# Attention row sums moved from TensorE to GpSimd for four of eight heads, with three other moves, in a one-core encoder kernel

## What is computed

```python
def attend(q_blk):
    s = jnp.einsum('bqhd,bkhd->bhqk', q_blk, k).astype(jnp.float32) * scale
    prob = jax.nn.softmax(s, axis=-1)
    return jnp.einsum('bhqk,bkhd->bqhd', prob.astype(v.dtype), v)
...
sa = jnp.einsum('bhvk,bhk->bhv', S, a_t)
S_new = S * w_t[:, :, None, :] + sa[..., None] * b_t[:, :, None, :] + v_t[..., None] * k_t[:, :, None, :]
```

## Time and profile before

| | us |
|---|---|
| three runs | 1579.66, 1581.14, 1581.53 |
| median | 1581.14 |
| the profiled execution, its time | 1581.29 |
| its span in the profile | 1579.4 |
| TensorE busy | 1525.7 (97%) |
| VectorE busy | 1051.0 (67%) |
| ScalarE busy | 636.6 (40%) |
| GpSimd busy | 349.3 (22%) |
| mean granted TensorE clock | 0.995 of full speed |

### The profile page before, as it was taken

One profiled execution on the slowest core, in us unless ns is written; L12 is line 12 of the kernel. 1 busy time (PEld: TensorE's weight loads), 2 busy tenths in 40 slices (PEclk: granted clock), 3 DMA queues, 4 the chain that ended last, 5 costly groups with the idle time before them and its releaser, 6 DMA issues.

```text
span 1579.4 us, 25838 instructions
## 1 busy us (share of the span) xinstructions
PE 1525.7 (97%) x10160; PEld 1104.2 (70%) x10160; DVE 1051.0 (67%) x1503; ACT 636.6 (40%) x1178; POOL 349.3 (22%) x356
## 2 busy tenths in 40 slices
PE   6999999999999999999999999999999999999998
PEld 5888776644555546777764457888888888888786
DVE  6424589678666676666548489875555555689877
ACT  5212247645444444444430125433333333343553
POOL 0810013146100028887830050220000000000000
PEclk9999999999999999999999999999999999999999
DMA  6141020010000000000033011333221111765322
GB/s 244 45 155 53 20 63 5 7 28 13 12 12 24 7 18 16 2 2 29 2 129 126 1 53 54 114 115 118 81 80 54 54 54 54 260 207 196 124 67 107
DMA packets 29001, 110.70 MB, mean 70 GB/s; under 512 B 3568, under 2 KB 6096, under 8 KB 26720
## 3 DMA queue, kind: packets, MB, share of 16 engines
q1 hardware_dynamic: 28432, 103.97, 19.5%
q0 software_dynamic: 464, 5.28, 0.8%
HBM read 89.36 MB, written 18.92 MB: 69 GB/s over the span
## 4 chain that ended last, share of the span: by engine, by line
PE 72%; issue 12%; DVE 9%; POOL 5%; ACT 2%; DMA 1%; DVEq 0%; SPq 0%; POOLq 0%; ACTq 0%
PE psum L2909 25%; PE psum L2926 12%; PE psum L2833 7%; PE psum L2579 4%; PE psum L2606 3%; PE psum L2497 2%; PE psum L2613 1%; PE psum L2516 1%; PE psum L2467 1%; POOL arena L853 1%; POOL arena L855 1%; PE psum L2807 1%; PE psum L2720 1%; PE psum L2716 1%; PE psum L2702 1%
## 5 line engine op out<-in xcount | busy, mean ns | idle before, releaser
L1988 DVE TENSOR_TENSOR part_lo<-arena,part_hi 128x512 fp32r<-128x512 f32 x154 | 117.7, 768 | 77.2 <-ACT part_hi L1269 77.0
L2909 PE MATMUL psum<-h_hi,part_hi 128*128 128x512 f32 x616 | 165.7, 391 | 1.1 <-ACT arena L1317 0.7
L2909 PE MATMUL psum<-h_lo,part_hi 128*128 128x512 f32 x616 | 164.7, 389 | 0.0
L2909 PE MATMUL psum<-h_hi,part_lo 128*128 128x512 f32 x616 | 164.7, 389 | 0.0
L1269 ACT ACTIVATE part_hi<-arena 128x512 fp32r<-128x512 f32 x154 | 95.9, 628 | 133.3 <-PE psum L2909 114.8
L2909 PEld LDWEIGHTS psum<-h_hi,part_hi 128*128 128x128 f32 x616 | 115.2, 188 | 26.7 <-ACT arena L1317 1.1
L2909 PEld LDWEIGHTS psum<-h_lo,part_hi 128*128 128x128 f32 x616 | 115.6, 188 | 24.1
L2909 PEld LDWEIGHTS psum<-h_hi,part_lo 128*128 128x128 f32 x616 | 115.6, 188 | 24.0
L919 POOL TENSOR_TENSOR arena<-arena,consts 128x512 f32<-128x512 f32 x64 | 81.8, 1299 | 179.9 <-ACT arena L1170 179.3
L1658 DVE TENSOR_REDUCE stats<-psum 128x1 f32<-128x1024 f32 x64 | 77.8, 1216 | 51.1 <-PE psum L2497 51.0
L2833 PE MATMUL psum<-arena 128*128 128x512 f32 x256 | 110.5, 592 | 0.0
(11 more groups left out here) (329 smaller groups left out, 3046.7 us busy)
## 6 DMA issues: line engine op xcount, KB each, us to landing
arena<-in_w_gate SPq DMA_DIRECT2D x22, 512.0 KB, 3.7
arena<-in_w_up SPq DMA_DIRECT2D x22, 512.0 KB, 3.8
arena<-in_w_down SPq DMA_DIRECT2D x22, 512.0 KB, 3.7
arena<-in_w_down SPq DMA_DIRECT2D x11, 1024.0 KB, 4.9
arena<-in_w_in SPq DMA_DIRECT2D x15, 512.0 KB, 3.5
arena<-act_spill SPq DMA_DIRECT2D x12, 512.0 KB, 7.1
act_spill<-arena SPq DMA_DIRECT2D x10, 512.0 KB, 6.1
arena<-in_x SPq DMA_DIRECT2D x8, 512.0 KB, 8.5
```

Of the source, the lines that this page charges most:

```text
L1988: v.tensor_tensor(lo, raw[:, at:at + HALF], hi, ALU.subtract).then_inc(part_lo, 1)
L2909: mm = pe.matmul(bank({2: z, 3: y, 5: y}.get(p, x)), w[:, P * k:P * k + P], h[k // 2][:, HALF * (k % 2):HALF * (k % 2) + HALF], start=(fre ...
```

## The change

Four edits:

1. **Sums.** For heads 4 to 7, GpSimd adds the exponentials of the eight key tiles elementwise into one 128x1024 buffer (`e_sums`): seven additions a head, counted by `summed`. In head 7 it adds six tiles (five additions). TensorE then needs four matmuls with ones for a whole head (`sums_of`) in place of 64, between scores 0 and 1 of the next head; for head 7 it runs them ahead of `values` 6, and the last two tiles are added by TensorE as before. ScalarE now also waits for `summed` ahead of writing a ring buffer. VectorE inverts the sums of heads 4 to 6 when scores 1 of the next head are done. The loops over these heads are written out on PE, ACT and DVE.
2. **Decayed operands.** `At` and `Rt` of `q` 0 and 1 are made in head 6, behind the row maxima 3 and 4 (`decayed`), and no longer in head 7.
3. **GpSimd's order.** The five operations of `q` now wait for the first scores of head `q`.
4. **Start.** The identity matrix is loaded behind the first four row tiles.

```diff
@@ -295,6 +295,8 @@
+        SUMMED = 4
+        e_sums = [reg(X0 + 6144, T), reg(WK0 + 3200, T)]
...
@@ -643,8 +645,7 @@
         def _(sp):
             for t in range(4):
                 sp.dma_start(resid[:, t, :], a["x"][t]).then_inc(rows_in_place[t], 16)
-                if t == 0:
-                    sp.dma_start(ident, a["consts"][:, 0:P]).then_inc(ident_in, 16)
+            sp.dma_start(ident, a["consts"][:, 0:P]).then_inc(ident_in, 16)
             for s in range(NSLOT):
...
             pool.wait_ge(z_sig, 14)
             pool.wait_ge(kk_ready, 2)
-            pool.wait_ge(s_done, 1)
             for q in range(4):
                 hp = q % 2
+                pool.wait_ge(s_done, 8 * q + 1)
                 own.add(pool.tensor_tensor(Bt[:, q], Kt[:, q], kk[:, hp], ALU.mult))
                 own.wait()
                 own.add(pool.tensor_scalar(Kt[:, q], Kt[:, q], pcol("k_a", hp), one_less_ka[:, hp:hp + 1],
@@ -907,6 +908,15 @@
                 own.add(pool.tensor_tensor(Bt[:, q], Bt[:, q], half[q % 2], ALU.mult))
                 own.wait()
                 pool.tensor_tensor(Kt[:, q], Kt[:, q], half[q % 2], ALU.mult).then_inc(kb_ready, 1)
+
+            pool.wait_ge(kb_ready, 4)
+            for n in range(HEADS - SUMMED):
+                total = e_sums[n % 2]
+                for kt in range(1, NT if n < HEADS - SUMMED - 1 else NT - 2):
+                    pool.wait_ge(e_ready, 8 * (SUMMED + n) + kt + 1)
+                    if kt > 1:
+                        pool.wait_ge(summed, 7 * n + kt - 1)
+                    pool.tensor_tensor(total, e_ring[0] if kt == 1 else total, e_ring[kt % NE], ALU.add).then_inc(summed, 1)
 
             pool.wait_ge(prods_ready, PRODS[3])
             def level(d, m, i):
...
@@ -1170,13 +1180,17 @@
...
-            def head_exps(i, b, ahead, ahead2, with_decays=False, last=False):
+            def head_exps(i, b, ahead, ahead2, with_decays=False, last=False, add_up=False):
...
                         act.wait_ge(pv_done, 8 * i + (4 * b + (kt - NE) // 2 + 1))
+                    if add_up and (kt >= NE or first_summed < 2 * i + b):
+                        n = 2 * i + b - first_summed
+                        act.wait_ge(summed, 7 * n + max(kt - NE, 1) if kt >= NE else 7 * (n - 1) + kt + NE)
                     at = 2 * (1 - kt % 2)
                     act.activation(halves(e_ring[kt % NE]), psum[:, at:at + 2, :], ACT.Exp, scale=MLA_SCALE).then_inc(e_ready, 1)
                 if ahead:
...
@@ -1721,9 +1735,12 @@
                         row_max(*nxt, kt)
                     beside(kt)
 
-            def invert(i, b, last=False):
-
-                v.wait_ge(pv_done, 8 * i + (4 * b + 4))
+            def invert(i, b, last=False, add_up=False):
+
+                if add_up and 2 * i + b < HEADS - 1:
+                    v.wait_ge(s_done, 8 * (2 * i + b + 1) + 2)
+                else:
+                    v.wait_ge(pv_done, 8 * i + (4 * b + 4))
                 v.reciprocal(inv_own[last][b], bank(7, 256)).then_inc(inverted, 1)
 
             def scale_pair(i, last=False):
...
 
-            def recurrence_operands():
-
-                v.wait_ge(max_ready, HEADS)
+            def decayed(q):
+
+                hp = q % 2
+                v.wait_ge(pr_q, HEADS)
                 v.wait_ge(pr_v, HEADS)
-                v.wait_ge(s_done, 8 * (HEADS - 1))
                 v.wait_ge(kb_ready, 4)
                 v.wait_ge(ex_ready, 16)
+                if q < 2:
+                    v.tensor_tensor(by_chunk(At[:, q])[:, :, 0], by_chunk(kk[:, hp])[:, :, 0], lead[:, q],
+                                    ALU.mult).then_inc(prods_ready, 1)
+                    v.tensor_tensor(by_chunk(At[:, q])[:, :, 1:P], by_chunk(Rt[:, q])[:, :, 0:P - 1],
+                                    by_chunk(kk[:, hp])[:, :, 1:P], ALU.mult).then_inc(prods_ready, 1)
+                else:
+                    v.tensor_tensor(At[:, q], Rt[:, q], kk[:, hp], ALU.mult).then_inc(prods_ready, 1)
+                v.wait_ge(prods_ready, PRODS[q] - 1)
+                v.tensor_tensor(Rt[:, q], Rt[:, q], r_sh[:, hp], ALU.mult).then_inc(prods_ready, 1)
+
+            def recurrence_operands():
+
+                v.wait_ge(max_ready, HEADS)
+                v.wait_ge(s_done, 8 * (HEADS - 1))
                 for q in range(4):
                     hp = q % 2
-                    if q < 2:
-                        v.tensor_tensor(by_chunk(At[:, q])[:, :, 0], by_chunk(kk[:, hp])[:, :, 0], lead[:, q],
-                                        ALU.mult).then_inc(prods_ready, 1)
-                        v.tensor_tensor(by_chunk(At[:, q])[:, :, 1:P], by_chunk(Rt[:, q])[:, :, 0:P - 1],
-                                        by_chunk(kk[:, hp])[:, :, 1:P], ALU.mult).then_inc(prods_ready, 1)
+                    if q >= 2:
+                        decayed(q)
                     else:
-                        v.tensor_tensor(At[:, q], Rt[:, q], kk[:, hp], ALU.mult).then_inc(prods_ready, 1)
-                    v.wait_ge(prods_ready, PRODS[q] - 1)
-                    v.tensor_tensor(Rt[:, q], Rt[:, q], r_sh[:, hp], ALU.mult).then_inc(prods_ready, 1)
-                    if q < 2:
-                        v.wait_ge(prods_ready, PRODS[q])
+                        v.wait_ge(prods_ready, PRODS[1])
                         v.scalar_tensor_tensor(out=bonus[hp], in0=Kt[:, q], scalar=pcol("r_k", hp), in1=Rt[:, q],
                                                op0=ALU.mult, op1=ALU.mult).then_inc(rk_ready, 1)
 
...
+                        invert(i, 0, last=True, add_up=True)
                         recurrence_operands()
...
-            def values(i, b, first):
+            def sums_of(i, b):
+
+                last = 2 * i + b == HEADS - 1
+                pe.wait_ge(summed, 7 * (2 * i + b - SUMMED + 1) - 2 * last)
+                pe.wait_ge(inverted, 2 * i + (b + 2))
+                for g in range(4):
+                    mm = pe.matmul(bank(7, 256, slice(32 * g, 32 * g + 32)), cst(C_ONES)[:, 0:32],
+                                   e_sums[b][:, 256 * g:256 * g + 256], start=True, stop=not last, skip_group_check=True)
+
+            def values(i, b, first, add_up=False):
...
+                if first == 0 and not add_up:
                     pe.wait_ge(inverted, 2 * i + (b + 2))
-                for kt in (first, first + 1):
+                for kt in () if add_up and (i, b, first) != (HEADS // 2 - 1, 1, 6) else (first, first + 1):
                     for g in range(4):
...
                 scores(i, b, 0, ahead)
+                if left_over is not None:
+                    sums_of(*left_over)
                 scores(i, b, 1, ahead)
...
                     pe.wait_ge(e_ready, 8 * HEADS)
                     attention(PLAN[1])
-                values(i, b, 6)
+                    sums_of(i, b)
+                values(i, b, 6, add_up)
...
-            with pe.Fori(0, HEADS // 2 - 1) as i:
+            with pe.Fori(0, SUMMED // 2) as i:
                 for b in range(2):
                     head(i, b, True, True)
-            for b in range(2):
-                head(HEADS // 2 - 1, b, b == 0, False)
+            for h in range(SUMMED, HEADS):
+                before = ((h - 1) // 2, (h - 1) % 2) if h > SUMMED else None
+                head(h // 2, h % 2, h < HEADS - 1, h < HEADS - 2, add_up=True, left_over=before)
```

More of the change, by code:

```diff
@@ L1816, in _ @@
             pair(0, None)
[L1817 to L1820 removed]
+            for i in range(1, HEADS // 2 - 1):
+                pair(i, i - 1)
             pair(HEADS // 2 - 1, HEADS // 2 - 2, last=True)
```

42 lines of the change are left out of this document (20 added, 22 removed).

## The result

The changed kernel takes 1585.82 us (median of seven runs, 1582.23 to 1587.40); the kernel before, run beside it, 1580.11 (seven, 1576.88 to 1582.40). The ratio is 1.0039, 95% interval 1.0028 to 1.0049: 6 us slower, where 1582.6 was forecast. That is within the range, but on the slow side of the 0.2% that the prediction called no change. The profiled execution took 1585.09 with a span of 1583.3, 3.9 more than before.

The account below looks back on a forecast made before the run. TensorE's instruction stream (72% of the span) was taken to set the pace. Heads 4 and 5, head 6, head 7, clock, order, start: -6.6 + 3.7 + 7.5 + 3.2 - 6.0 - 0.5 = +1.3 on 1581.29, so 1582.6; range 1568 to 1591.

Parts of the forecast that it names:

- who holds whom: Latent attention: two-SBUF-input VectorE instructions and GpSimd's never run together; they alternate at 1.1 us and 1.9 us a sum.
- VectorE is not held twice: Rival, chance 0.28: head 6 loses 2.5 instead of 6.0, head 7's operands end at 14 instead of 21; 1570.
- heads 4 and 5, -6.6 predicted: Each head 33.10 - 3.67 for fewer ones + 0.35 for late guard 3 = 29.8, so -6.6 for two.
- head 6, +5.3 with its clock: Head 6: the same saving, less cover 0.98 and 6.0 for decayed operands: 32.0, +3.7, before the clock's share.
- its clock: Heads 6 and 7: TensorE at 1.2 GHz behind new waits, two stretches, +3.2 together (0 to 5).
- The early keys themselves: Head 6: decayed operands between row maxima 3 and 5 take guards 3 to 7 to 15.7 against 10.1; 6.0 taken.
- the dear-sums rival: Rival, chance 0.16: a GpSimd sum takes 2.2 or more, delaying guards 4 and head 7; +5.8, clock +1.5, 1590.
- Head 7, +7.5 and 1.6 of clock predicted: Head 7: VectorE's operands, alternating with five sums, end at 21; the first chunk's second block at 30.3, before 22.0; +7.5.
- The 0.8 that was taken off for the second block: Head 7: some 0.8 that GpSimd took from the second block before, taken off +8.3 to give +7.5.
- the order and the start: GpSimd's order in heads 1 and 2, -6.0 (-3 to -7.5); identity load at the start, -0.5 (0 to -1).
- the price that was put on head 1 for `q` 1: Head 1: VectorE still waits for two products of `q` 1, making guards 5 and 6 late by 1.1 together.
- the 0.8 kept for chance: Order term of heads 1 and 2: 0.8 for a chance of a slow stretch, within the -6.0.

Follow-up runs that it names:

- writes_only: The changed kernel with GpSimd's additions replaced by fills of the same buffer, which read nothing: 1565.83 us, ratio 0.9909.
- The swaps: Two kernels, the kernel before with GpSimd's two residual operations exchanged, or their gain and bias rows instead: 2.00 us with the bias row, 2.40 with the gain row.
- sums_4to6_late: The changed kernel with sums in heads 4 to 6 only, decayed operands back in head 7, VectorE's turned-query split behind row maxima 3: 1565.83 us, ratio 0.9912.
- order_only: The kernel before with only GpSimd's order changed, each q waiting for the first scores of head q: 1572.49 us, ratio 0.9955.
- start_only: The kernel before with only the identity matrix loaded behind the first four row tiles: 1576.78 us, ratio 0.9986.
- order_start: The kernel before with both GpSimd's new order and the later identity load, no sums and no early keys: 1571.39 us, ratio 0.9952.
- decayed_in_7: The changed kernel with the decayed operands of q 0 and 1 made in head 7 again: 1583.01 us, ratio 1.0025.

## Why the prediction went as it did

**Right: who holds whom.** VectorE and GpSimd took turns for as long as both had work: 3.1 to 3.4 us a pair in head 7, `attention(PLAN[1])` waiting for VectorE (3.90), one decayed instruction of 3.25 in head 6, the clock under 0.97 in both heads, heads 1 and 2 clean. "VectorE is not held twice" is out by the same rows, and writes_only shows that the loss lies in GpSimd's reading additions: their turns with VectorE and, not separated from them, their length. The Trainium skill ("SBUF — State Buffer", Who interferes with whom) gives the rule that was used; each row above agrees with it.

**Wrong: heads 4 and 5, -6.6 predicted, -3.3 measured.** Three numbers of this step failed, of which the first is the large one: guard 4's waits, 1.12 and 0.88, are 2.0 of the 3.3.
- A sum was priced at 2.00, from the earlier trace rows, because the row there was the same operation. The swaps show that the operation had nothing to do with it. A sum in the heads costs 2.38 (median of 26), as the products of the earlier trace rows do. Then the third sum ends beyond the point where the scores 4 and 5 hide VectorE's subtraction, and guard 4 is 1.1 late. The step said that these scores hide it, also for a wait of up to 1.9. That does not come out of its own numbers: 1.9, 1.1 for the subtraction and 1.2 for the row maximum are 4.2, and from guard 3 to where guard 4 could start are 3.5 (464.67 to 468.19). sums_4to6_late, where the wait is gone, has heads 4 and 5 at 30.03 and 30.76, beside the predicted 29.8.
- `sums_of` was priced at 0.25, a quarter of a group of ones. A group is eight calls of `matmul`, which the trace counts as x16, and `sums_of` is four: half a group. From scores 0 to scores 1 head 5 takes 2.17 with it and head 4 1.50 without: 0.67 for each of heads 5 to 7, and nothing in head 4, so 0.67 in these two heads for the 0.5 put down. The words on the change ahead of the prediction, four matmuls in place of 64, counted calls on one side and the trace's instructions on the other; it is 4 for 32, or 8 for 64. The row in head 5:

```profile
487.83 0.64 PE L2628 MATMUL psum<-arena,consts 128*32 128x256 f32 x8
```

- A group of ones that is gone was priced at 0.98. It gives 0.87: the values ahead of it are followed by the next instruction after 1.85 us (469.97 to 471.82 in head 4), where the ones followed after 1.74. Three such groups a head are 0.7 in both heads. Some 0.4 more is spread over small waits and not traced.

**Wrong: head 6, +5.3 with its clock, +8.0 measured.** Without the early keys it was taken at 25.97 (28.31 less 3.67, plus 0.35 and 0.98) and takes 27.80: the same errors, guard 4 (0.9), `sums_of` (0.4) and the values' end (0.3), carry 1.6 of 1.8. The early keys themselves were 6.0 and 1.6 of clock, 7.6, and measured 8.5. But neither part was as told. There is one wait of 4.25 ahead of guard 5 and none of its kind ahead of guard 6, since GpSimd was through with sums 4 and 5 by 537.29; and the clock cost 4.1 (11.10 against 6.96 for the same matmuls). The wait was priced too high and the clock too low, and this nearly cancels. The 6.0 itself stood for a sum of 5.6 (15.7 less 10.1), without a reason for the rest. One thing here was the dear-sums rival's: sum 4 did start (531.58) ahead of the first decayed keys (532.70).

**Head 7, +7.5 and 1.6 of clock predicted, +9.8 measured.** The clock cost nothing on the path here: TensorE is slow only behind its wait of 3.90, when VectorE is what the first chunk waits for. So it is +7.5 that stands against +9.8. VectorE's operands end 23.0 behind the first scores and not 21: the inversion begins at 3.9 and not 3.1, part of it the dearer `sums_of`, and the five sums are 0.4 longer each, some of it hidden. The 0.8 that was taken off for the second block is shown by no row. The steps behind the operands take 8.8 in place of 9.3.

**Too small: the order and the start.** -6.0 was -7.6 in heads 1 and 2 (7.6 in order_only too): the price that was put on head 1 for `q` 1 and the 0.8 kept for chance did not fall due, head 1 came to 33.26. -0.5 was -1.7 up to the first scores, in one execution of each; start_only has 2.2 in all (0.6 to 4.0). The other 1.4 of heads 0 to 3 is head 0, where nothing had been put down. It goes with the granted clock, 0.95 in place of 0.91, and came and went in kernels with the same edits (order_start, above): that much is chance.

So the errors half cancel, by the rows of the table: +3.3 and +2.7 and +0.7 against -3.1 and -1.2 give 2.4 more than predicted; 0.2 more came behind. That they cancel is luck, and so is a part of the total's closeness; the mechanism, turns that cost more than TensorE saves, is not. Between these 3.9 and the 5.7 between the medians lie the executions: the profiled one of before was 1.2 over the median of its seven runs, that of after 0.7 under its own. The dear-sums rival had the right price of a sum, the early sum 4 and late guards 4 (0.5 said, 0.88 measured in heads 5 and 6), and put the total at 1590; order and start, at the forecast's values in it, are 4.3 of the difference to the measured time.

## What to carry to other kernels

Work given to GpSimd can cost VectorE its own length wherever VectorE reads two SBUF operands meanwhile: ask of each such instruction who waits for it, and put it behind the one that TensorE awaits (one line moved gave 3 us here) or keep those stretches free; two edits that are harmless apart (early keys, sums up to head 6) cost 8 to 9 us together, because TensorE pays for such a wait twice, in the changed kernel's head 6 with 4.3 us of waiting and 4.1 in matmuls at 1.2 GHz behind it. Take an instruction's price from more than one row, with different operands, and not from one row of the same name, and count both sides of a saving in the trace's units.

## What the runs showed of the hardware that was not expected

- GpSimd's two-input instruction on 128x1024 takes 2.00 or 2.40 us by which row is its second input, not by the operation. The gain row lies 1,026 columns ahead of the bias row in the same tensor; whether their places or their contents decide was not tried. The Trainium skill ("GPSIMD Engine Reference", Engine selection) has a two-input operation at about twice VectorE's time: 2.38 to 1.22 agrees, 2.00 does not.
- The smallest instructions of VectorE are held too: seven of 128x2 took 2.78 beside GpSimd's level mask and 0.58 in writes_only; a product of 128x8 took 1.85 and 2.34 beside sums (decayed_in_7) and 0.15 alone.
- The turns are not strictly one to one: behind the small held product (552.01, ended 553.86) the next of VectorE ran at once in 1.21, and only the one behind that was held.
- A fill by GpSimd beside VectorE's two-input instructions left them at 1.22.
